# Two-block kernel on one core: where the modulation product of the second block is formed

## The reference

```python
mod_l = (jax.nn.silu(c) @ w_mod[l] + b_mod[l])[:, None, :]
mod_c = (jax.nn.silu(c_ctx) @ w_mod[l] + b_mod[l])[None, None, :]
sh1, sc1, g1, sh2, sc2, g2 = jnp.split(mod_l, N_MOD, axis=-1)
sh1c, sc1c, g1c, sh2c, sc2c, g2c = jnp.split(mod_c, N_MOD, axis=-1)
pl = _modulate(_rmsnorm(xl, norm1_w[l]), sh1, sc1) @ w_in[l]
pc = _modulate(_rmsnorm(xc, norm1_w[l]), sh1c, sc1c) @ w_in[l]
```

## Time and profile before

| | us |
|---|---|
| median of 3 runs | 2077.9 |
| lowest, highest | 2074.66, 2089.6 |
| profiled execution | 2077.58 |
| its span, first to last instruction | 2075.7 |
| PE busy in it | 1926.9 (93%) |
| DVE busy in it | 1010.5 (49%) |
| mean granted TensorE clock | 0.952 of full |

### The profile page before, as it was taken

How to read it: one execution, slowest core, us unless ns; L and a number is a source line. 1 busy time by engine, 2 the same in 40 slices (tenths; PEclk the granted TensorE clock), 3 DMA queues, 4 the chain that set the end, 5 groups by cost and what they waited for, 6 DMA issues and landing times.

```text
span 2075.7 us, 20749 instructions
## 1 busy us (share of the span) xinstructions
PE 1926.9 (93%) x7602; PEld 1280.8 (62%) x7602; DVE 1010.5 (49%) x1877; ACT 700.4 (34%) x1142; POOL 401.1 (19%) x376
## 2 busy tenths in 40 slices
PE   7997779899999899999998998999998989999996
PEld 3556433333787687888773445666564558888874
DVE  5955332221444443244221315656575268777774
ACT  3261223422323343124124214361634153323323
POOL 2621100000200000000000011322222037555551
PEclk9995878999999999999999999999999989999999
DMA  5263342132433132332310221121201134242411
GB/s 134 82 98 95 110 146 81 62 101 76 128 91 111 61 101 81 101 100 84 100 61 1 76 57 41 46 56 31 61 21 41 42 103 122 79 122 68 116 41 41
DMA packets 203020, 164.55 MB, mean 79 GB/s; under 512 B 17527, under 2 KB 193379, under 8 KB 202667
## 3 DMA queue, kind: packets, MB, share of 16 engines
q1 hardware_dynamic: 197803, 149.21, 24.3%
q0 software_dynamic: 4576, 14.17, 3.3%
q10 hardware_dynamic: 560, 0.12, 0.0%
HBM read 153.78 MB, written 4.26 MB: 76 GB/s over the span
## 4 chain that ended last, share of the span: by engine, by line
PE 80%; DVE 10%; ACT 4%; issue 3%; DMA 2%; ACTq 0%; POOLq 0%; POOL 0%; DVEq 0%; SPq 0%
PE bank L1387 25%; PE bank L1722 17%; PE bank L1484 9%; PE bank L1496 4%; PE bank L1277 4%; PE bank L1317 2%; PE bank L1331 2%; DVE arena L2382 2%; PE bank L1169 2%; PE bank L1609 2%; PE bank L1601 2%; PE bank L1083 1%; DMA ring<-in_w_mod 1%; PE bank L1253 1%; PE bank L1077 1%
## 5 line engine op out<-in xcount | busy, mean ns | idle before, releaser
L3189 DVE SCALAR_TENSOR_TENSOR arena<-bank,ffn_taps,arena 128x441 f32<-128x441 f32 (+2 forms) x352 | 220.0, 684 | 81.0 <-ACT arena L2344 81.0
L2752 DVE TENSOR_TENSOR w_lo<-ring,w_hi 128x2048 fp32r<-128x2048 f32 x52 | 119.2, 2292 | 166.0 <-ACT w_hi L1949 161.9
L1484 PE MATMUL bank<-hT,ring 128*128 128x512 f32 x448 | 197.5, 594 | 0.0
L1387 PE MATMUL bank<-h_lo,w_hi 128*128 128x512 f32 x448 | 176.5, 394 | 8.1 <-ACT arena L1986 4.9
L1949 ACT CAST w_hi<-ring 128x2048 fp32r<-128x2048 f32 x52 | 99.1, 1906 | 192.0 <-PE bank L1387 192.0
L1387 PE MATMUL bank<-hT_hi,w_hi 128*128 128x512 f32 x384 | 151.6, 395 | 5.6 <-DVE h_lo L2826 5.6
L1722 PE MATMUL bank<-hT_hi,w_hi 128*128 128x512 f32 x352 | 138.5, 393 | 9.9 <-DVE h_lo L3167 9.9
L1484 PEld LDWEIGHTS bank<-hT,ring 128*128 128x128 f32 x448 | 84.0, 191 | 97.5 <-issue 97.3
L1387 PE MATMUL bank<-act_hi,w_hi 128*128 128x512 f32 x352 | 137.8, 391 | 5.4 <-DVE act_lo L2838 5.4
L1033 POOL TENSOR_TENSOR w_lo<-ring,w_hi 128x2048 fp32r<-128x2048 f32 x22 | 101.7, 4624 | 187.9 <-ACT w_hi L2318 124.7
L1722 PE MATMUL bank<-h_lo,w_hi 128*128 128x512 f32 x352 | 138.0, 392 | 0.0
(11 more groups left out here) (455 smaller groups left out, 3674.3 us busy)
## 6 DMA issues: line engine op xcount, KB each, us to landing
ring<-in_w_up SPq DMA_DIRECT2D x76, 512.0 KB, 4.6
ring<-in_w_mod SPq DMA_DIRECT2D x48, 512.0 KB, 4.6
ring<-in_w_in SPq DMA_DIRECT2D x72, 256.0 KB, 3.3
ring<-in_w_down SPq DMA_DIRECT2D x32, 512.0 KB, 4.0
ring<-in_w_in SPq DMA_DIRECT2D x30, 512.0 KB, 4.1
arena<-in_w_down SPq DMA_DIRECT2D x22, 512.0 KB, 4.5
ring<-in_w_out SPq DMA_DIRECT2D x8, 512.0 KB, 4.1
ring<-in_w_out SPq DMA_DIRECT2D x16, 256.0 KB, 3.0
```

Source lines behind the costliest of these rows:

```text
L1387: ins = pe.matmul(out, u[:, n % SLOTS, cols], v[:, k, :], start=start and k == w[0][0] and m == 0, stop=stop and k == w[-1][0] and m == 2)
L1484: ins = pe.matmul(o, w[:, k, :], src[:, k, 0:n], start=k == 0, stop=k == DT - 1)
L2752: ve.tensor_tensor(w_lo[:, n % SLOTS, :], ring[:, n % SLOTS, :], value(w_hi[:, n % SLOTS, :]), ALU.subtract)\
L3189: return ve.scalar_tensor_tensor(o[:, ys, xs], x[:, yt, xt], ffn_taps[:, at:at + 1], o[:, ys, xs], ALU.mult, ALU.add)
```

## The change

The products with the slabs move from PE to DVE. DVE multiplies each of the 8 steps of a slab (128 x 256) by the silu value of its partition and adds them up in `mod_sums`; this is `sum_mod`. For the first 8 slabs, of which both modulations are needed, there are two such sums (16 instructions a slab), for the other 16 only one, kept in two alternating halves (8 instructions a slab). PE then only sums over the partitions: four matmuls a slab with the sums as weights (128 x 128) and a column of ones as the moving operand, so that the result lies as columns in bank 2 and stays there. The copies of the rows, their 24 stores, the reload, the transposition and the semaphores of these go. The three first slabs are summed in score units 1 to 4, 7 to 10 and 13 to 16, two steps a unit; the 21 others in halves of items 0 to 63, `mod_part`, 1.3 steps a half: one half ahead of `part_mask` and one behind it. SP loads slab c when slab c - 2 has been summed (`mod_summed`) and no longer when PE has started on it. DVE waits before slab c for PE to have taken slab c - 2 (`mod_taken`). The bias is added by DVE at item 67, and the last `glu` waits for that, as it uses bank 2.

The diff, without declarations, bounds of the arena and the count in `started`:

```diff
-MOD_AFTER = {1: 0, 3: 1, 5: 2, 9: 3, 11: 4, 13: 5, 15: 6, 17: 7}
+MOD_FIRST = {1: 0, 7: 1, 13: 2}
+MOD_AFTER = {n + 4: c for n, c in MOD_FIRST.items()}
 UNIT_AT = {s: FIRST + 2 + s // 2 for s in range(0, 2 * (FIRST - 2), 2)}
-CMP_MODS = 8
-MOD_AT = {3 + 4 * k: 9 + k for k in range(8)} | {37 + 4 * k: 17 + k for k in range(7)}
+BOTH_MODS = 2 * DT // 2
+MOD_PARTS, MOD_HALVES = DT * (MODS - 3), 128
+MOD_AT = {(DT * (c - 2) - 1) * MOD_HALVES // MOD_PARTS // 2 + 2: c for c in range(3, MODS)}
+MOD_DONE = max(MOD_AT) + 2
...
-        mod_rows = rstd[0:2].rearrange("p (k n) -> p k n", k=2)
+        mod_sums = ptmp.rearrange("p k (v n) -> p k v n", v=2)
...
-        mod_bank = banks[2][0:2, 0:2 * P]
+        mod_bank = banks[2][:, 2 * P:2 * P + (NMOD + 2) * DT]
...
-            def store_mod(c):
-
-                sp.wait_ge(mod_out, c + 1)
-                sp.dma_start(mod_scr[:, c * width:(c + 1) * width], mod_rows[:, c % 2]).then_inc(mod_stored[c % 2], 16)
-
             for c in range(MODS):
-                columns(C0["mod"] + c, a["w_mod_2"][0], c * width, width)
-                if c:
-                    store_mod(c - 1)
+                if c == 1:
+                    sp.wait_ge(hid_full, 2)
+                elif c:
+                    sp.wait_ge(mod_summed, c - 1)
+                columns(C0["mod"] + c, a["w_mod_2"][0], c * width, width, free=c > 0)
             g = C0["glu"]
             w_glu = a["ssm_w_glu"][0].rearrange("(k p) n -> p k n", p=P)
             dst = ring[:, g % SLOTS, :].rearrange("p (k n) -> p k n", k=UT)
-            load(g, (dst[:, 0:2], w_glu[:, 0:2]), (dst[:, 2:4], w_glu[:, 2:4]))
-            store_mod(MODS - 1)
+            sp.wait_ge(mod_summed, MODS - 1)
+            load(g, (dst[:, 0:2], w_glu[:, 0:2]), (dst[:, 2:4], w_glu[:, 2:4]), free=True)
+            sp.wait_ge(mod_summed, MODS)
+            skipped[0] += MODS
...
-            for k in range(2):
-                pool.wait_ge(mod_stored[k], 16 * MODS // 2)
-            pool.dma_start(mod_back[0:2 * NMOD * DT], mod_scr.rearrange("c (m p) -> (c m) p", p=P)).then_inc(mod_in, 16)
...
-                if g:
-                    pe.wait_ge(mod_out, CMP_MODS)
...
             def modulation(c):
 
-                n = C0["mod"] + c
-                arrived(n)
-                if c in (0, CMP_MODS):
-                    pe.wait_ge(c_read, 1 + (c > 0))
-                if c:
-                    pe.wait_ge(mod_out, c)
-                w = slot(n)
-                for k in range(DT):
-                    ins = pe.matmul(mod_bank, silu_c[:, k, :], w[:, k, :], start=k == 0, stop=k == DT - 1)
-                    if k == 0:
-                        ins.then_inc(chunk_used, 1)
-                ins.then_inc(mod_full, 1)
+                if c == 0:
+                    pe.wait_ge(c_read, 1)
+                if c == len(MOD_AFTER):
+                    pe.wait_ge(c_read, 2)
+                pe.wait_ge(mod_summed, c + 1)
+                both = c < BOTH_MODS
+                for v in range(2 if both else 1):
+                    for k in range(2):
+                        at = v * NMOD * DT + 2 * c + k
+                        parts = (v,) if both else (0, 1)
+                        for part in parts:
+                            ins = pe.matmul(mod_bank[:, at:at + 1], mod_sums[:, c % 2, part, k * P:(k + 1) * P], one[:],
+                                            start=part == parts[0], stop=part == parts[-1])
+                ins.then_inc(mod_taken, 1)
...
-                    pe.wait_ge(mod_out, MODS)
+                    pe.wait_ge(mod_ready, 1)
...
-            modulation(CMP_MODS)
...
-            pe.wait_ge(mod_in, 16)
-            flip(banks[5][:, 0:2 * NMOD * DT], mod_back[0:2 * NMOD * DT], 2 * NMOD * DT).then_inc(mod_flipped, 1)
...
-            def mod_copy(c):
-
-                ve.wait_ge(mod_full, c + 1)
-                if c >= 2:
-                    ve.wait_ge(mod_stored[c % 2], 16 * (c // 2))
-                ve.tensor_copy(mod_rows[:, c % 2], mod_bank).then_inc(mod_out, 1)
+            def sum_mod(c, steps):
+
+                n = C0["mod"] + c
+                both = c < BOTH_MODS
+                w = ring[:, n % SLOTS, :].rearrange("p (k n) -> p k n", k=DT)
+                for k in steps:
+                    if k == 0:
+                        if c == 0:
+                            ve.wait_ge(silu_ready, 2)
+                        ve.wait_ge(loaded[n % SLOTS], 32 * (n // SLOTS + 1))
+                        if c >= 2:
+                            ve.wait_ge(mod_taken, c - 1)
+                    for v in range(2 if both else 1):
+                        total, weigh = mod_sums[:, c % 2, v if both else k % 2], silu_c[:, k, v:v + 1]
+                        if k < (1 if both else 2):
+                            ins = ve.tensor_scalar(total, w[:, k, :], weigh, None, ALU.mult)
+                        else:
+                            step.wait(step.base + step.n - 1)
+                            ins = ve.scalar_tensor_tensor(total, w[:, k, :], weigh, total, ALU.mult, ALU.add)
+                        if k == DT - 1 and (v or not both):
+                            step.wait(step.base + step.n)
+                            ins.then_inc(mod_summed, 1)
+                        else:
+                            step.mark(ins)
+
+            def mod_part(h):
+
+                for at in range(-(-h * MOD_PARTS // MOD_HALVES), min(-(-(h + 1) * MOD_PARTS // MOD_HALVES), MOD_PARTS)):
+                    sum_mod(3 + at // DT, (at % DT,))
+
+            def mod_biased():
+
+                ve.wait_ge(mod_taken, MODS)
+                b = vec[:, VEC["b_mod_2"]:VEC["b_mod_2"] + NMOD * DT]
+                n = NMOD * DT
+                step.mark(ve.tensor_tensor(mod[:, 0:2 * DT, 1], mod_bank[:, n:n + 2 * DT], b[:, 0:2 * DT], ALU.add))
+                ve.tensor_tensor(mod[:, :, 0], mod_bank[:, 0:n], b, ALU.add).then_inc(mod_ready, 1)
...
             for n in range(FIRST + 2):
                 maxima(n)
+                for at, c in MOD_FIRST.items():
+                    if at <= n < at + 4:
+                        sum_mod(c, range(2 * (n - at), 2 * (n - at) + 2))
...
-            mod_copy(MOD_AFTER[FIRST + 1])
...
-            mod_copy(CMP_MODS)
...
             for s in range(ITEMS):
+                mod_part(2 * s)
                 if s % (2 * PARTS) == 0 and s:
...
                 if s + AHEAD < ITEMS:
                     part_mask(s + AHEAD)
-                if s - 1 in MOD_AT:
-                    mod_copy(MOD_AT[s - 1])
+                mod_part(2 * s + 1)
+                if s == MOD_DONE:
+                    mod_biased()
                 if s in UNIT_AT:
                     maxima(UNIT_AT[s])
...
-            ve.wait_ge(mod_flipped, 1)
-            b = vec[:, VEC["b_mod_2"]:VEC["b_mod_2"] + NMOD * DT].unsqueeze(2).to_broadcast([P, NMOD * DT, 2])
-            ve.tensor_tensor(mod[:], banks[5][:, 0:2 * NMOD * DT].rearrange("p (c m) -> p m c", c=2), b, ALU.add)\
-              .then_inc(mod_ready, 1)
```

More of the change, by code:

```diff
@@ L77 @@
 BANKS, SLOTS = 4, 2
-ARENA = 34 * 1024 - 160
+ARENA = 34 * 1024 - 192
 (LOG_DT, DT_, AR_DT, ANGLE, TURNS, SIN_H, SIN, COS, MAG, MAG_STEP, DEN, NR, FR, FI, TMP, _1, _2, _3, _4) = range(19)
@@ L288, in two_block_program @@
         zero = sb("zero", [P, 1])
+        one = sb("one", [P, 1])
         same = sb("same", [P, len(LEVELS), P], U8)
@@ L415, in two_block_program @@
         block_of = area(W2 + 4 * K, P)
-        mod_back = area(W2 + 4 * K + P, P)
-        assert W2 + 4 * K + 2 * P <= ARENA - 160
+        assert W2 + 4 * K + P <= ARENA
         weight_at, at2 = {}, 0
@@ L487, in two_block_program @@
         u_scr = nc.dram_tensor("u_scr", (UT * P, STEP, CHUNKS), F32, kind="Internal").ap()
-        mod_scr = nc.dram_tensor("mod_scr", (2, NMOD * D), F32, kind="Internal").ap()
         y_scr = nc.dram_tensor("y_scr", (UT * P, STEP, CHUNKS), F32, kind="Internal").ap()
@@ L507, in two_block_program @@
             sem(n) for n in ("s5_full", "y_copied", "y_out", "y_in", "y_sum", "gelu_done", "glu_sig", "yssm_ready"))
-        silu_ready, mod_full, mod_out, mod_in, mod_flipped, mod_ready = (
-            sem(n) for n in ("silu_ready", "mod_full", "mod_out", "mod_in", "mod_flipped", "mod_ready"))
-        mod_stored = [sem(f"mod_stored{k}") for k in range(2)]
+        silu_ready, mod_summed, mod_taken, mod_ready = (
+            sem(n) for n in ("silu_ready", "mod_summed", "mod_taken", "mod_ready"))
         kv_in, blocks_ready = sem("kv_in"), sem("blocks_ready")
@@ L629, in started @@
         def started(name):
-            return C0["mix"] + CHUNK_AT[name] - SPLITS1 + 1
+            return C0["mix"] + CHUNK_AT[name] - SPLITS1 + 1 - MODS
         mix_loaded = [loaded[0], up_in[0], loaded[1], up_in[1]]
@@ L653, in _, with load @@
             skipped = [0]
-            def load(n, *pairs, i=0, per=0, split=None):
-                if split is not None:
+            def load(n, *pairs, i=0, per=0, split=None, free=False):
```

(6 more changed lines are left out.)

## The result

| | before | after |
|---|---|---|
| median, us (4 runs each, same chip) | 2080.95 | 2133.71 |
| lowest, highest | 2074.66, 2089.6 | 2130.0, 2135.44 |
| profiled execution, span | 2077.58, 2075.7 | 2132.02, 2130.2 |
| mean granted clock in it | 0.952 | 0.897 |

The change makes the kernel slower: the ratio of after to before is 1.0248, 95% interval 1.0205 to 1.0291. It is 53 us on the medians and 54.5 us between the two profiled spans, which are compared from here on. A profile is one execution, and starts of a stage differ by some us between executions.

A forecast was written before the change was run, and what follows sets the result against it. The prediction took the attention stage to be bound by PE, with the granted clock deciding. From 2077.6 us it took 5 for earlier items, added 43 for items 0 to 63 and 2 for glu: forecast 2117 us, range 2030 to 2142.

The forecast's parts named there:

- Items 0 to 63: Attention stage: 240 us against 197, +43 us, with one fifth of the stage at full clock.
- the stage wholly at half clock: Items 0 to 63 without any clock rise until glu: 262 us, whole kernel 2140 us; a rival, chance 0.22.
- The claim that rises happen only inside a modulation: From 204 to 435 us: eleven clock rises, each inside a modulation, none inside score units, parts or values.
- The rival of full clock: Items 0 to 63: steady items lift and hold the clock, stage 150 us, whole kernel 2026 us; chance 0.18.
- The rival of DVE as the bound: Items at mostly full clock, 0.685 us a sum: stage 190 us, whole 2066 us, or 2040 to 2095; chance 0.20.
- The sums: New DVE work on the slabs: 208 instructions at 0.406 us, 84 us, plus 14 us of tensor_scalar, together 98 us.
- The work that stays on PE: Four one-column matmuls a slab, 8 records: 1.7 us at half clock or 0.84 at full, against 3.54 before.
- The items: Their start, after the score units: some 5 us earlier than before.
- The end of the stage: First glu after the items: runs at half clock before its own products lift it, +2 us.
- The GLU load and the merge load: They wait for slabs 22 and 23: both have time; if not, the price is one load, under 5 us.
- The rest: Beyond items and score units: glu +2 us; stores, reload, late transposition and bias add 0, with 1 us gain as other bound.

The follow-up runs named there:

- the restoring runs: Changed kernel with 8 unread 192-column matmuls behind each of the 21 modulations in the items: 2120.93 us; with steps 2 to 5 of each slab's sums omitted: 2130.26 us.

## Why the prediction was right, and where it wasn't

**The mechanism held.** The forecast was that taking the streams away takes the clock away, and that the stage then loses more to the clock than the modulations it sheds. Items 0 to 63 were put at 240 us and took 241. That the two agree so closely is luck, for the sizes behind it were off in both directions: one fifth of the stage at full clock was assumed and about a tenth had it (mean 0.55), and the stage wholly at half clock was put at 262 us, while the kernel with half the sums needed 246 with a clock of 0.50 and 0.55. With a tenth instead of a fifth its own sum would have given 251 us. The steps that the restoring runs tested stand: streams that do nothing raise the clock, less work on DVE doesn't help.

**The claim that rises happen only inside a modulation was too narrow.** Its count of eleven rises is right, but in the changed kernel there is no modulation of the old kind left, and the clock still rose, at 352 us amid values and parts, and at 437 us during the transposes of four rows, which I had counted as working against it. Both times it was back at 0.50 within some 11 us. What raised it there stays open.

**The rival of full clock** needed steady work to lift the clock. PE was busy in 194 of 197 us at 0.55, and in 86.00 of 86 us at 0.50 from 448 us on. The Trainium skill ("TensorE: Matmul & The Clock Gate", section "Why this matters for your kernels") asks for a TensorE that is kept continuously busy; by this trace that is not enough where about half of the time goes to matmuls over 64 or 67 of the 128 rows.

**The rival of DVE as the bound** was right in its condition: nothing of it at half clock, and 9.84 of 10 us busy once 128-row parts bring the clock up. The price was lower than its 190 us: 164 us for items 0 to 63 in that kernel, and a sum takes 0.431 us of DVE (89.7 / 208), not 0.685. The sums cost 105 us against 98 forecast: 90 for 84, and 15.3 for 14.

**The work that stays on PE** was put at 1.7 us a slab at half clock: 1.5 to 1.8 in the chain. **The items** were to begin 5 us earlier and began 8 earlier; with only the tile `one` moved they begin at 298.6 us instead of 292.75, so the 3 us mean little. **The end of the stage** was +2 for the first glu. From the first glu to the second it is 8.8 us instead of 6.7, and all that follows is as long as before: +2. The GLU load and the merge load, which I gave nothing with a bound of under 5 us, cost nothing that the chain shows.

**The step that failed is "The rest".** It gave nothing to all that follows, and 17 of the 54 us arose there. The declaration of `one` was left out of the diff shown and out of the costs; it is 4 bytes a partition, and what it moved costs as much as a third of the whole result. Up to the first fp32r product the chain shows +38 us where my sum had +40, so nearly all of the difference between 2117 and the 2134 us measured is this one term.

**What the change would have been worth.** With parts of 128 rows on both sides and no shift, the kernel with the sums on DVE takes 2039.0 us and the one with the modulation on PE 2063.0, 1.2% less on the medians. The two ran on different chips, but their ratios to the kernel before, 0.9770 [0.9732, 0.9809] and 0.9916 [0.9882, 0.9949], don't overlap. So the exchange of work pays, once the clock doesn't hang on the work that is given away.

## What to carry to other kernels

Before work is moved off TensorE, look at which of its matmuls the granted clock rises in, and ask what is left to lift it; the products here took 1.9 times as long at half clock (2.01 us against 1.05), whatever was saved. Matmuls with few rows can be let run over zeroed rows, which cost no time of TensorE here (1.05 us at full clock with either) and won 75 us in one kernel and 21 in the other. Put new small tiles behind the large operands, or compare the addresses of both versions: the runs of unchanged code in the chain are the check. The last and longest of them took 337.91 to 337.95 us in all six kernels in which nothing was shifted.

## What was not expected of the hardware

- The address of fp32r operands matters. Shifted up by 32 bytes, the same 1476 records take 345.7 us instead of 337.9 (2.3%), by 64 bytes 346.8. Runs of plain float32 matmuls took what they had (27.66, 41.20 and 20.85 us).
- Rows that multiply zeros raise the mean clock (0.55 to 0.82 and more with 128 rows, 0.63 and 0.76 with 96). A record of the 512-column parts took 0.703 us on average with 128 rows and 1.048 with 67, by the clock alone.
- The same kernel varies from execution to execution, and the mean clock goes with it: the kernel before by 27 us in 19 executions (2067.1 at 0.957, 2093.6 at 0.946), the one with 96 rows by 28 us in eight (2072.8 at 0.924, 2101.0 at 0.914).
